# Three parts of the last down matrices, each loaded as 80, 40 and 8 rows

## What is computed

```python
    def expert_block(args):
        x_blk, e = args
        return (jax.nn.silu(x_blk @ w_gate[e]) * (x_blk @ w_up[e])) @ w_down[e]
```

## Time and profile before

| | before |
|---|---|
| median of 3 timed runs | 1019.05 us (1018.35 to 1020.17) |
| the profiled execution | 1018.47 us |
| its span, first to last instruction | 1016.6 us |
| TensorE busy | 972.3 us (96%) |
| DMA, all queues | 301.45 MB, mean 297 GB/s |
| mean granted TensorE clock | 0.987 |

### The profile page before, as it was taken

One profiled execution on the slowest core, in us unless ns is written; L12 is line 12 of the kernel. 1 busy time (PEld: TensorE's weight loads), 2 busy tenths in 40 slices (PEclk: granted clock), 3 DMA queues, 4 the chain that ended last, 5 costly groups with the idle time before them and its releaser, 6 DMA issues.

```text
span 1016.6 us, 15593 instructions
## 1 busy us (share of the span) xinstructions
PE 972.3 (96%) x6473; PEld 541.7 (53%) x6473; DVE 417.9 (41%) x807; ACT 189.3 (19%) x426; POOL 30.5 (3%) x92
## 2 busy tenths in 40 slices
PE   9999999999999999999999999999989998989997
PEld 8788866576666665468764533333323233333332
DVE  4576556175555555302232654722213122222213
ACT  2525344210000001214342100111101011101111
POOL 8200000000000000000000000000000000000000
PEclk9999999999999999999999999999989999999999
DMA  9443022775666689552144899999999999999994
GB/s 354 181 153 104 3 83 83 284 315 207 284 281 284 280 339 392 224 231 95 72 166 161 316 403 431 425 427 428 425 426 425 429 427 427 428 426 429 413 416 183
DMA packets 30386, 301.45 MB, mean 297 GB/s; under 512 B 6000, under 2 KB 6128, under 8 KB 12016
## 3 DMA queue, kind: packets, MB, share of 16 engines
q1 hardware_dynamic: 30320, 300.49, 72.1%
HBM read 299.43 MB, written 1.05 MB: 296 GB/s over the span
## 4 chain that ended last, share of the span: by engine, by line
PE 75%; DMA 13%; SPq 6%; DVE 3%; ACT 1%; issue 1%; ACTq 0%; DVEq 0%; POOL 0%; POOLq 0%
PE PS L1694 11%; PE PS L1295 10%; PE PS L2042 10%; PE PS L1290 9%; PE PS L1743 8%; DMA slot<-in_moe_w_up_dram 8%; PE PS L2061 6%; SPq L694 6%; DMA AR<-in_moe_w_up_dram 4%; PE PS L2018 3%; PE PS L1525 2%; PE PS L1641 2%; DMA slot<-in_moe_w_down_dram 1%; PE PS L1737 1%; PE PS L1993 1%; PE PS L1879 1%
## 5 line engine op out<-in xcount | busy, mean ns | idle before, releaser
L1694 PE MATMUL PS<-XH,slot 128*128 128x256 f32 x512 | 113.3, 379 | 1.7 <-DVE XH L2611 0.9
L1694 PEld LDWEIGHTS PS<-XH,slot 128*128 128x128 f32 x512 | 97.1, 190 | 21.3 <-issue 8.9
L1290 PE MATMUL PS<-XH,slot 128*128 128x256 f32 x432 | 97.8, 383 | 0.5 <-DVE XH L2294 0.5
L1290 PEld LDWEIGHTS PS<-XH,slot 128*128 128x128 f32 x432 | 80.7, 190 | 13.1 <-issue 1.2
L2042 PE MATMUL PS<-slot,ATT 128*32 128x512 f32 x544 | 68.6, 621 | 10.8 <-DMA slot<-in_moe_w_gate_dram 5.0
L2061 PE MATMUL PS<-slot,ATT 128*32 128x512 f32 x576 | 67.8, 618 | 7.0 <-DMA slot<-in_moe_w_up_dram 7.0
L1295 PE MATMUL PS<-slot,XH 128*128 128x256 f32 (+4 forms) x224 | 71.7, 476 | 0.0
L2042 PE MATMUL PS<-slot,MASKS 128*32 128x512 f32 x576 | 64.3, 594 | 1.0 <-DMA slot<-in_moe_w_down_dram 0.5
L2660 DVE SCALAR_TENSOR_TENSOR AR<-AR 128x384 f32<-128x384 f32 (+1 forms) x112 | 59.9, 610 | 0.0
L2018 PE MATMUL PS<-AR,DIAG 128*128 128x512 f32 x120 | 57.5, 604 | 0.0
L1295 PEld LDWEIGHTS PS<-slot,XH 128*128 128x128 f32 x224 | 42.0, 190 | 26.1 <-issue 14.8
(11 more groups left out here) (488 smaller groups left out, 1212.3 us busy)
## 6 DMA issues: line engine op xcount, KB each, us to landing
slot<-in_moe_w_up_dram SPq DMA_DIRECT2D x18, 2048.0 KB, 24.2
slot<-in_w_ffn_dram SPq DMA_DIRECT2D x16, 2048.0 KB, 8.4
slot<-in_moe_w_gate_dram SPq DMA_DIRECT2D x16, 2048.0 KB, 34.5
slot<-in_moe_w_down_dram SPq DMA_DIRECT2D x16, 2048.0 KB, 34.7
AR<-in_ada_w_dram SPq DMA_DIRECT2D x16, 1536.0 KB, 14.2
AR<-in_moe_w_gate_dram SPq DMA_DIRECT2D x9, 2048.0 KB, 27.7
AR<-in_moe_w_down_dram SPq DMA_DIRECT2D x8, 2048.0 KB, 31.6
AR<-in_moe_w_up_dram SPq DMA_DIRECT2D x8, 2048.0 KB, 35.3
```

Of the source, the lines that this page charges most:

```text
L1290: ins = pe.matmul(dst, w[:, c * width + col:c * width + col + n], HT[:, c, :], start=(c == 0), stop=(c == KC - 1))
L1694: ins = pe.matmul(PS[:, b, (f % 2) * T:(f % 2 + 1) * T], slots[s][:, c * 512 + f * P:c * 512 + (f + 1) * P], HT[:, c, :], start=(c == 0), ...
```

## The change

Parts 1, 2 and 3 of the last pair's down matrices are no longer loaded with one transfer of 128 rows for each matrix, but with three, of rows 0 to 79, 80 to 119 and 120 to 127. The loop over the row ranges is the innermost, so a matrix's three transfers are issued one behind the other, and then those of the other matrix. Part 0 stays one transfer of 128 rows. All transfers of a part count up the same semaphore, so TensorE waits for 96 in place of 32. Bytes, columns and matmuls stay as they are.

```diff
         PARTS = {(NM - 2, 1): 2, (NM - 2, 2): 2, (NM - 1, 0): 2, (NM - 1, 1): 4, (NM - 1, 2): 4}
+        LAST_ROWS = ((0, 80), (80, 120), (120, P))
...
-                        sp.dma_start(part(RING[u % NR]), part(matrix(kind, experts[k]))).then_inc(part_loaded[m, kind][f], 16)
+                        for r0, r1 in LAST_ROWS if (m, kind) == (NM - 1, 2) and f > 0 else ((0, P),):
+                            sp.dma_start(part(RING[u % NR])[r0:r1], part(matrix(kind, experts[k]))[r0:r1])\
+                                .then_inc(part_loaded[m, kind][f], 16)
...
-                pe.wait_ge(part_loaded[m, 2][f], 32)
+                pe.wait_ge(part_loaded[m, 2][f], 32 * (len(LAST_ROWS) if m == NM - 1 and f > 0 else 1))
```

## The result

The changed kernel takes 1026.9 us (median of 4 runs, 1025.72 to 1028.27), the kernel before 1018.7 us (median of 4, 1017.33 to 1020.17). The ratio is 1.0081, 95% interval 1.0064 to 1.0098: +8.2 us. The forecast was 1022.3 with a range to 1026.0, so the direction was right and the size too small.

What follows compares the result with a forecast made beforehand. The expert weight stream was taken to bound the kernel, TensorE following. Sharing of ways into memory, +3.3 us with the load's +0.5 inside and issuing hidden, on 1019.05 gave 1022.3 us, whole range 1018.2 to 1026.0.

Steps and rivals of the forecast that it cites:

- What bounds, and what there is to win: In the last down product, TensorE follows the expert weight stream; an earlier landing could win 0.48 us at most.
- Issuing: On SP, twelve more down transfers at 0.38 us each add 4.6 us, hidden behind engines still at work.
- The cover: The slowest engines' backlog at the last down issues, more than 10 us, was to hide SP's extra issue time.
- Shares of the engines: In parts 1 to 3, eight engines carry 10 rows, two 9, six 5, instead of 8: -0.48 to +1.9 us.
- way-in term: Writes of parts 1 to 3 into SBUF: engines sharing neighbouring rows halve each other; +3.3 us taken.
- load term: Uneven rows per engine in parts 1 to 3: +0.5 us by itself, counted within the +3.3 us for sharing.
- The way in: Engines writing neighbouring SBUF rows in parts 1 to 3 slow each other: 0 to +8.2 us, 40% taken, +3.3.
- the middles: Midpoints of the time ranges for 80, 40 and 8 rows: 2.64 us a set against 1.28, so +1.36.
- the upper end: Sharing over the six sets of parts 1 to 3 with nothing overlapping: +8.2 us.
- Relief: Rival, last down parts: memory does not bind and late engines are the six with 5 rows; 1018.6 us, chance 0.20.
- pile-up: Rival, last down parts: memory does not bind, late engines get more rows; +1.0 to +1.9 us, chance 0.20.
- no effect: Rival, parts 1 to 3: the queue cuts every transfer evenly, the last part lands as before; 1019.05 us, chance 0.08.

Runs made afterwards that it cites:

- e3: Parts 1 to 3 cut into even and odd rows, two transfers of 64 spread rows each, against the kernel before: ratio 0.9998.
- e2: Eighteen transfers over all 128 rows, cut by columns (640, 320 and 64 of 1024), against the kernel before: ratio 1.0002.
- e10: The changed kernel, with SyncE also waiting for part 0 to land before issuing part 1, so engines start in step; ratio to the kernel before 1.0076.
- e9: Parts 1 to 3 cut into 80, 32 and 16 rows, 8 rows on every engine, against the kernel before: ratios 1.0070 and 1.0061.
- e5: Parts 1 to 3 cut into 64, 32 and four times 8 rows, all spread apart, 36 transfers, against the kernel before: ratio 1.0099.
- the halves: Parts 1 to 3 cut into rows 0 to 63 and 64 to 127, twelve transfers, against the kernel before: ratios 1.0055 and 1.0053.
- m1: A kernel of transfers only, no computation, timing sixteen pieces per stage: 23.03 us for 128 rows, 36.40 us for 80, 40 and 8.

## Why the prediction was right and wrong

- **What bounds, and what there is to win.** Right. DMA paces the parts, and no kernel got under before by more than the noise: e3 still had 0.29 us of the wait, and its ratio is 0.9998.
- **Issuing.** Twelve more transfers were put at +4.6 us of SP, hidden. They took 20.43 - 10.73 = 9.7 us, and were hidden: e2 issues as many in 19.56 us at no cost. The price of one was about right: in e10, where the queue is empty, the eighteen pieces go out in 8.07 us, 0.45 each, and e9 needs 15.15 us for as many transfers as the change, +4.4. The rest of the 9.7 us is waiting for room in a slower queue, as far as these two say. The cover was named rightly, and e5 shows it gone.
- **Shares of the engines.** The counts 16, 10 and 8 were right. The sentence that let the way-in term hold the load term is the second step that failed, as far as is known. Out of step something adds about 3 us where +1.9 at most was given; if it is the load, an engine with 12 rows more, at half the rate, would need up to 2 x 1.9 us for them (an estimate).
- **The way in.** Mechanism, place and signature were right (half rate at a full share). The size was made of two mistakes that pull apart. By the middles a set was to cost 1.36 us more; in step it costs 0.84, since its pieces overlap. Then the first step failed: 60% was taken off for overlap by the engines' different progress, with nothing in the rows to size it. There is no such gain: the halves cost 5.4 to 5.6 us out of step and 5.6 by the rate. **This is the mis-sized term: 3.3 forecast, 5.0 by the rate alone, 8.2 measured, of which about 3 come on top of the rate.** That the upper end came to +8.2 as well is chance.
- **Where the time goes.** Parts 1 and 2 were to land a third and two thirds later and part 0 not at all. In truth part 0 started 5.8 us late, the up parts waited before it, and part 3's own wait was 1.11 us where 3.8 was forecast. I followed what waits behind the changed transfers, and forgot what is still in work on the late engines while the early ones are already at them.
- **Rivals.** Relief, pile-up and no effect all fell as first causes. Pile-up may be a part of the sum, and only beside sharing.
- **Chances and range.** 0.50 on slower by over 0.2% was the largest of the three and came true. The range ended 0.9 us short: it stopped at 1026.0, under the 1026.4 that the text itself gives as the forecast's own upper end, and although it had worked out 8.2 for no overlap.

## What to carry to other kernels

Don't cut a transfer into ranges of neighbouring rows: 64 neighbours take as long as all 128. Cut it by columns, or by every second row, which cost nothing in this kernel (every second row 7% at the bare rate, 24.65 us against 23.03). A queue of transfers has no single front: when engines differ by microseconds, a bad transfer also slows those issued ahead of it. And where a price is bounded only from far off, a kernel of transfers alone gives it: m1 had +5.0 us for the six sets.

## What the runs showed of the hardware

- The shared side is the one that is written: 37.87 us to neighbouring rows from spread ones, 25.80 the other way round.
- TensorE can come back from a wait slower. In the changed kernel it did nothing from 996.5 to 998.0 us and the granted clock in the next stretch was 0.58; 32 matmuls took 3.21 us there, after 2.81 us of waiting, and 1.93 before it. Not each wait does it: after 2.55 us ahead of part 1 the 16 matmuls took 1.92. In e10, after 4.14 us of waiting, 16 matmuls took 3.64 us in place of 1.92:

```profile
1007.18 3.64 PE L2047 MATMUL PS<-slot,MASKS 128*32 128x512 f32 x16 [4.14 <-DMA slot<-in_moe_w_down_dram]
```

  That is the lower of the clock's two levels, 1.2 GHz in place of 2.4. It adds nothing to the change's end, since the next part had not landed yet when these products were done, and part 3 ran at the full clock (1.92 us).
- SP's issuing of spread, narrow pieces can be the bound: 37 in 30.96 us in e5 (0.84 each, with the engines run dry), and m1's eleventh stage 96 in 64.71 us (0.67 each, at a DMA share of 0.44), about twice the 0.38 that was taken as the price from the earlier trace rows.
